# Attention scores in two sets of three PSUM banks, one maximum per unit, and a weight split moved to the output stage

## The reference

```python
def diff_scores_to_out(qb, k, v, lam):
    s = jnp.einsum('bhiqd,bhikd->bhiqk', qb, k, preferred_element_type=jnp.float32) * (HEAD_DIM ** -0.5)
    p = jax.nn.softmax(s, axis=-1)
    p_diff = p[:, :, 0] - lam * p[:, :, 1]
    return jnp.einsum('bhqk,bhkd->bhqd', p_diff.astype(v.dtype), v)
```

## Time and profile before

| | |
|---|---|
| median of three runs | 2636.8 us |
| the profiled execution | 2638.57 us |
| its span | 2636.7 us |
| TensorE busy | 2554.9 us (97%) |
| VectorE busy | 2069.8 us (79%) |
| ScalarE busy | 1012.5 us (38%) |
| loop and tail of attention, layer 0 | about 778 to 870 us |
| loop and tail of attention, layer 1 | about 2155 to 2224 us |
| granted TensorE clock there | 1.00 of full speed |

### The profile page before, as it was taken

The page is one execution under the profiler, slowest core; times in us unless marked ns, Lnnn a source line. Parts: engine busy times, 40 slices in busy tenths (PEclk is TensorE's granted clock), DMA queues, the critical chain, the costliest instruction groups (busy, mean ns, idle before and its releaser), DMA issues. The chain is left out here.

```text
span 2636.7 us, 42699 instructions
## 1 busy us (share of the span) xinstructions
PE 2554.9 (97%) x15356; PEld 2363.0 (90%) x15356; DVE 2069.8 (79%) x3414; ACT 1012.5 (38%) x1854; POOL 163.7 (6%) x314
## 2 busy tenths in 40 slices
PE   6999999999997999999999899999998998999999
PEld 5899999988965889999999799999997866989998
DVE  5688888887958388888888888777768956688885
ACT  4333433333147333422332433234324256344443
POOL 2000000020003200000000200000002003100001
PEclk8999999999999999999999999999999999999999
DMA  8234323332111113333334123343232201223332
GB/s 295 64 120 136 116 92 114 124 104 64 55 57 49 33 56 105 117 93 115 123 103 136 48 90 119 98 130 119 91 104 72 88 24 47 79 83 109 99 101 79
DMA packets 192361, 253.97 MB, mean 96 GB/s; under 512 B 7278, under 2 KB 130268, under 8 KB 192220
## 3 DMA queue, kind: packets, MB, share of 16 engines
q1 hardware_dynamic: 192220, 252.07, 30.4%
HBM read 249.95 MB, written 2.10 MB: 96 GB/s over the span
## 5 line engine op out<-in xcount | busy, mean ns | idle before, releaser
L1211 PE MATMUL ps<-h_hi,w_hi 128*128 128x384 f32 (+2 forms) x2368 | 790.5, 334 | 21.9 <-DVE h_lo L2326 18.2
L1213 PE MATMUL ps<-h_hi,w_lo 128*128 128x384 f32 (+2 forms) x2368 | 785.3, 332 | 0.0
L1212 PE MATMUL ps<-h_lo,w_hi 128*128 128x384 f32 (+2 forms) x2256 | 749.3, 332 | 0.0
L1211 PEld LDWEIGHTS ps<-h_hi,w_hi 128*128 128x128 f32 x2368 | 449.3, 190 | 53.6 <-issue 22.5
L1213 PEld LDWEIGHTS ps<-h_hi,w_lo 128*128 128x128 f32 x2368 | 449.3, 190 | 20.7
L1212 PEld LDWEIGHTS ps<-h_lo,w_hi 128*128 128x128 f32 x2256 | 428.0, 190 | 19.2 <-issue 1.0
L1811 ACT ACTIVATE w_hi<-raw 128x512 fp32r<-128x512 f32 x464 | 279.7, 626 | 420.8 <-PE ps L1213 327.8
L2468 DVE TENSOR_TENSOR w_lo<-raw,w_hi 128x512 fp32r<-128x512 f32 x464 | 307.5, 684 | 14.8 <-ACT w_hi L1811 14.8
L1211 PE MATMUL ps<-t_hi_all,w_hi 128*128 128x384 f32 x864 | 292.1, 338 | 0.0
L1213 PE MATMUL ps<-t_hi_all,w_lo 128*128 128x384 f32 x864 | 292.0, 338 | 0.0
L1212 PE MATMUL ps<-t_lo_all,w_hi 128*128 128x384 f32 x864 | 291.9, 338 | 0.0
(11 more groups left out here) (276 smaller groups left out, 3994.1 us busy)
## 6 DMA issues: line engine op xcount, KB each, us to landing
side_raw<-in_w_ada SPq DMA_DIRECT2D x240, 256.0 KB, 2.7
raw<-in_w_ffn_gate SPq DMA_DIRECT2D x44, 1024.0 KB, 5.4
raw<-in_w_ffn_up SPq DMA_DIRECT2D x44, 1024.0 KB, 5.4
raw<-in_w_ffn_down SPq DMA_DIRECT2D x44, 1024.0 KB, 5.0
raw<-in_w_in SPq DMA_DIRECT2D x14, 1024.0 KB, 5.3
ada_buf<-in_w_ada SPq DMA_DIRECT2D x12, 1024.0 KB, 12.4
raw<-in_w_out SPq DMA_DIRECT2D x8, 1024.0 KB, 5.7
raw<-in_w_in SPq DMA_DIRECT2D x8, 512.0 KB, 7.2
```

The lines of the kernel that those rows point to most:

```text
L1211: mm(out, wh, xh, start=start, stop=False, skip_group_check=reopened)
L1212: mm(out, wh, xl, start=False, stop=False, skip_group_check=reopened)
L1213: return mm(out, wl, xh, start=False, stop=stop, skip_group_check=reopened)
```

## The change

1. `score_sets` takes the place of `score_slots`. Banks 0 to 2 are set 0 and banks 3 to 5 are set 1. Units 0 and 1 use set 0, unit 2 set 1, unit 3 set 0, and so on in turn. A score waits for both exponents of the unit that had the set last, two units back in the loop.
2. A latent unit's 2 x 768 scores lie packed in the three banks of a set. The calls are stream 0 with keys 0 to 511, stream 1 with keys 0 to 255, stream 1 with keys 256 to 767, stream 0 with keys 512 to 767. The second and the fourth write the two halves of the middle bank, and the fourth waits on a new semaphore, `early_keys`, until the second is done.
3. Both maxima of a latent unit come from one instruction over 2 x 768 values. Both exponents wait for it.
4. The Fourier and convolution products take banks 3 to 7 in turn instead of 4 to 7. The first score waits for banks 0 to 2, and `attention` at its start for banks 3, 4 and 5.
5. The split of output tile 2 leaves the attention loop (steps 10 and 11) and stands behind it, ahead of the split of tile 3 on ScalarE and ahead of the first residual additions on VectorE.

```diff
-def score_slots(l):
-    ...
+def score_sets(l):
+
+    out, last = [], {}
+    for i in range(len(units_of(l))):
+        mine = 0 if i < EARLY_UNITS else (i + 1) % 2
+        out.append((mine, 2 * last[mine] + 2 if mine in last else 0))
+        last[mine] = i
     return out
...
-        banks = itertools.cycle(range(4, 8))
+        banks = itertools.cycle(range(3, 8))
...
-                for b in range(4):
+                for b in range(3):
                     pe.wait_ge(bank_free[b], plan.before_scores[l][b])
...
                 if s == 0:
-                    parts = [(st, 2 * mine[st] + half, 384 * half, 384) for half in range(2) for st in range(2)]
+                    parts = [(0, 0, 0, 0, 512), (1, 1, 256, 0, 256), (1, 2, 0, 256, 512), (0, 1, 0, 512, 256)]
                 else:
-                    parts = [(st, 2 * mine[0] + st, LAT, CTX) for st in range(2)]
-                for st, b, ko, n in parts:
+                    parts = [(st, st, 0, LAT, CTX) for st in range(2)]
+                for st, b, at_, ko, n in parts:
                     r = slice(64 * st, 64 * st + 64)
-                    last = mm(ps[:, b, 0:n], qT[r, h, o:o + 128], kT[r, h, ko:ko + n],
+                    if s == 0 and (st, b) == (0, 1):
+
+                        pe.wait_ge(early_keys, latents_before(l, i) + 1)
+                    last = mm(ps[:, 3 * mine + b, at_:at_ + n], qT[r, h, o:o + 128], kT[r, h, ko:ko + n],
                               start=True, stop=True, skip_group_check=True)
+                    if s == 0 and (st, b) == (1, 1):
+                        last.then_inc(early_keys, 1)
                 last.then_inc(products, 1)
...
-                for b in (4, 5):
+                for b in (3, 4, 5):
                     pe.wait_ge(bank_free[b], plan.before_att[l][b])
...
-                    act.wait_ge(max_done, maxima_before(l, i) + (st + 1 if s == 0 else 1))
+                    act.wait_ge(max_done, u_before + i + 1)
...
-                    if i in (4, 7, 10):
-                        split(("out", l, (4, 7, 10).index(i)))
+                    if i in (4, 7):
+                        split(("out", l, (4, 7).index(i)))
+                split(("out", l, 2))
                 split(("out", l, 3))
...
                     if s == 0:
-                        for st in range(2):
-                            dve_.reduce_max(nb[:, p, st:st + 1], ps[:, 2 * mine[st]:2 * mine[st] + 2, 0:384], AX.XY,
-                                            negate=True).then_inc(max_done, 1)
+                        both = pflat[:, 512 * bank:512 * bank + 2 * TOK].rearrange("p (s n) -> p s n", s=2)
                     else:
-                        dve_.reduce_max(nb[:, p, :], ps[:, 2 * mine[0]:2 * mine[0] + 2, 0:CTX], AX.X,
-                                        negate=True).then_inc(max_done, 1)
+                        both = ps[:, bank:bank + 2, 0:CTX]
+                    dve_.reduce_max(nb[:, p, :], both, AX.X, negate=True).then_inc(max_done, 1)
...
-                    if i in (5, 8, 11):
-                        split(("out", l, (5, 8, 11).index(i)))
+                    if i in (5, 8):
+                        split(("out", l, (5, 8).index(i)))
+                split(("out", l, 2))
```

More of the change, by code:

```diff
@@ L149, in units_of, with latents_before @@
     return [(h, s, t) for h in range(HEADS) for s in range(len(mix_segs(l))) for t in range(mix_segs(l)[s][1] // 128)]
-def score_slots(l):
[L154 to L161, removed]
-    return out
-def maxima_before(l, i):
-    return sum(2 if s == 0 else 1 for x in range(l) for h, s, t in units_of(x)) \
-        + sum(2 if s == 0 else 1 for h, s, t in units_of(l)[:i])
+def score_sets(l):
[4 more added lines that the diff above has]
+        last[mine] = i
+    return out
+def latents_before(l, i):
+    return sum(s == 0 for x in range(l) for h, s, t in units_of(x)) + sum(s == 0 for h, s, t in units_of(l)[:i])
 T_LAG, O_LAG, OT_LAG = 2, 3, 9
@@ L720, in trunk @@
         max_done = sem("max_done")
+        early_keys = sem("early_keys")
         exp_done = sem("exp_done")
@@ L1673, in score @@
                 h, s, t = units_of(l)[i]
-                mine, need = score_slots(l)[i]
+                mine, need = score_sets(l)[i]
                 if t == 0 and s == 0:
@@ L2096, in mix @@
                 u_before = units_before(l)
-                slots = score_slots(l)
+                sets = score_sets(l)
                 def copy_p(u, half):
@@ L2107, in exponent @@
                     h, s, t = us[i]
-                    mine = slots[i][0]
-                    act.wait_ge(max_done, maxima_before(l, i) + (st + 1 if s == 0 else 1))
+                    bank = 3 * sets[i][0]
+                    act.wait_ge(max_done, u_before + i + 1)
                     dst = e0[i % 3][:] if st == 0 else e1[i % 2][:]
                     if s == 0:
-                        dst = dst.rearrange("p (b n) -> p b n", b=2)
-                        src = ps[:, 2 * mine[st]:2 * mine[st] + 2, 0:384]
+                        at_ = 512 * bank + TOK * st
+                        src = pflat[:, at_:at_ + TOK]
                     else:
                         dst = dst[:, 0:CTX]
-                        src = ps[:, 2 * mine[0] + st, 0:CTX]
+                        src = ps[:, bank + st, 0:CTX]
                     act_fn(dst, src, ACT.Exp, bias=nb[:, i % 2, st:st + 1], scale=1.0,
@@ L2911, in maximum @@
                     wait_products(dve, ("score", l, i))
-                    p, mine = i % 2, score_slots(l)[i][0]
+                    p, bank = i % 2, 3 * score_sets(l)[i][0]
                     if s == 0:
-                        for st in range(2):
-                            dve_.reduce_max(nb[:, p, st:st + 1], ps[:, 2 * mine[st]:2 * mine[st] + 2, 0:384], AX.XY,
-                                            negate=True).then_inc(max_done, 1)
-                    else:
-                        dve_.reduce_max(nb[:, p, :], ps[:, 2 * mine[0]:2 * mine[0] + 2, 0:CTX], AX.X,
-                                        negate=True).then_inc(max_done, 1)
+                        both = pflat[:, 512 * bank:512 * bank + 2 * TOK].rearrange("p (s n) -> p s n", s=2)
+                    else:
+                        both = ps[:, bank:bank + 2, 0:CTX]
+                    dve_.reduce_max(nb[:, p, :], both, AX.X, negate=True).then_inc(max_done, 1)
                 def combine(i):
```

## The result

The changed kernel takes 2648.86 us, the median of 6 runs (2645.41 to 2652.16). Six runs of the kernel before gave 2637.72 (2636.55 to 2639.59). The ratio is 1.0042 [1.0032, 1.0052]: 11 us slower, where I forecast no change (2636.7, range 2631 to 2645). Its profiled execution took 2645.61 us, with a span of 2643.7.

A forecast was written before the change was run, and what follows sets the result against it. The prediction took a chain of waits, no full engine, to bound the attention stages, layer 1 being held by TensorE's order and bank 6. Terms of +1.5 (layer 1) and -1.6 (layer 0) gave -0.1: 2636.7 us, range 2631 to 2645.

The forecast's parts named there:

- the calls of a score: TensorE, latent scores: four unequal calls take 1.28 us as before, the fourth call's wait having 0.27 to spare; cost 0.
- slower rival, in order of issue: Latent scores on TensorE: records can't start before those issued ahead; +0.21 us a score, 6.7 in all, 2643.4; chance 0.18.
- maximum of a latent unit: VectorE: one maximum over 1536 values takes 1.75 us, where two instructions took 1.82.
- exponent behind it: ScalarE: the first exponent starts 1.79 us after the maximum's start instead of 0.99, so 0.80 later.
- layer 1, start of the loop: Layer 1: unit 2's score waits for the low part to empty bank 3, from 2155.34 to 2156.98: +1.6 us.
- layer 1, unit 2 to the first `turn_o`: Layer 1 attention loop: steps 3 to 5 give -0.3 us, steps 5 to 10 with two splits +0.2.
- pair of steps, but for the calls: Layer 1, `turn_o` to `turn_o`: the copy behind the later exponent adds 0.52 us, 8.30 becomes 8.82.
- third split, layer 0 and 1: Attention loops: without tile 2's split, layer 0 saves 1.25 us and layer 1 saves 1.56.
- a further head of layer 0: Layer 0, two more heads: later exponents delay low parts and the copy, +0.2 us a head, +0.4 in all.
- split behind the loop: Output stage: tile 2's split fits ScalarE's 2.34 us gap and VectorE has eight banks of cover; cost 0.
- layer 0 up to the first `turn_o`: Layer 0: scores and maxima come 1.5 us earlier, the later exponent gives 0.80 back: -0.75 us.
- The faster rival: Attention stages: the exponent's wait was the bound; all 9.1 us go plus the third split's savings, 2624.9; chance 0.10.

The follow-up runs named there:

- the kernel without the wait: The kernel before with calls of 512, 256, 512 and 256 keys, each stream in its own two banks, no second semaphore: 2638.09 us, ratio 1.0002.
- the second call first: The changed kernel with a latent score's first two calls exchanged, stream 1's 256 keys issued ahead of stream 0's 512: 2641.1 us, ratio 1.0015 to the kernel before.
- both maxima first: The kernel before, with a latent unit's first exponent waiting for both maxima, still two instructions, and three pairs of banks kept: 2659.2 us, ratio 1.0091.

## Why the prediction was wrong

The failed step is the calls of a score. I wrote that the fourth call "waits for the second, done at 0.11 + 2 x 0.21 + 0.16 = 0.69, and its turn is at 0.96, with 0.27 to spare". The end of the second call was right (0.705), and so was the turn. The wait, however, ended at 1.20, when the first call had ended. I had reckoned when the work is done, not when its end is told, and had taken two streams that run side by side as independent in both. It cost 0.33 us a score where the term said 0: 32 scores would be 10.6, of which 7.8 arrive. Of the rest a part is hidden on the way from unit 2 to the first `turn_o` of layer 1, where 8 scores added 34.96 - 33.57 = 1.4 us and not 2.6.

My slower rival, in order of issue, had the right direction and the right group of calls, but another mechanism and size. It let the starts be in order (+0.21, 2643.4); the starts were free, and the kernel without the wait shows that they cost nothing. Had I put the end of the first call in place of the second's, my own numbers would have given 0.11 + 2 x 0.43 + 0.16 = 1.13, and with 0.05 for the semaphore and the turn at 0.96 a loss of 0.22 a score: 32 x 0.22 = 7.0, or 2643.7.

The clock is a second miss: some 3.1 us that stood in no term and in no bound. By itself it would have left the time inside the range.

The other terms, by the prediction's own steps:

| step | forecast | measured |
|---|---|---|
| maximum of a latent unit | 1.75 | 1.76 |
| exponent behind it | 1.79 | 1.79 |
| layer 1, start of the loop | +1.6 | +1.63 |
| layer 1, unit 2 to the first `turn_o` | -0.1 | -0.09 |
| pair of steps, but for the calls | 8.82 | 8.83 |
| third split, layer 0 and 1 | -1.25, -1.56 | -1.25, -1.56 |
| a further head of layer 0 | +0.2 | +0.39 |
| split behind the loop | 0 | 0 |
| layer 0 up to the first `turn_o` | -0.75 | -0.75 to -1.35, estimated |
| the calls of a score | 0 | +0.33 each |

A head is 7.36 + 6.26 + 9.95 = 23.57 with the second call first, and 7.36 + 6.41 + 9.41 = 23.18 before. The last but one row can't be read directly: every profile with the new sets has the half-speed stretch just there (31.94 us with the second call first, 31.69 before without). Less the 1.0 to 1.6 us of a stretch (above), 30.3 to 30.9 is left, an estimate. The total of the terms was -0.1; by the rows of the second call first they add up to between -0.3 and +0.3, and at equal clock it was +0.5. One reading in the prediction was off without harm: the copy's room is not the 0.15 us that ScalarE stood idle before it but 0.27 (2206.62 less 2205.47 + 0.88), and the sum used 0.27 (0.80 became 0.52).

The faster rival fell as argued: with the exponent's wait gone the copy is late next. It was cheap to lift, though, by the order of instructions on ScalarE. With it the sets are worth -4.4 us at equal clock, and -7.1 with the split; the -11.9 of that rival was too high, but not empty.

## What to carry to other kernels

Before you make a matmul wait for another, ask which longer ones were issued ahead of that other: here its end was told no sooner than that of the long one, though that ran on the other half of the rows. Issue the call that is waited for first; here that was an exchange of two entries in a list, worth 7.8 us. And when a wait goes away, look at what stands behind the delayed instruction on its own engine: the copy had only the wrong place in line.

## What the runs showed of the hardware

- Two calls on different halves of the rows run unhindered with 512 and 256 columns side by side: first passes of 0.32 us beside first passes of 0.54, and 1.49 us for a whole score, as with equal calls of 384.
- A call of 256 columns raised its semaphore 1.15 us after the score's start and released the wait at 1.20, though its passes were over at 0.70; a call of 512 columns issued ahead of it ended at 1.12. Issued first, it raised the semaphore at 0.71 and released the wait by 0.75, with the long call still running.
- Starting again after that wait took some 0.1 us beyond the lateness. A wait that was over before the turn of its call's passes, and one more increment a score, cost nothing that shows: 1.49 us with them and without.
- A stretch of 3.4 us at half clock cost 1.0 to 1.6 us, and kernels with the same products got mean clocks from 0.9918 (both maxima first) to 0.9946 (before). This is as large as most of the effects looked for here, so effects of a few us had to be read stage by stage, or at equal clock.
